# The tail of a mixture-of-experts layer: half of the rank rows added by accumulating transfers

## What is computed

```python
h = h + g2 * _moe(u, ...)          # routed experts + shared expert
return _rmsnorm(h, final_g)

# _moe: 128 experts, each token goes to its top 8
routed = sum over the token's 8 experts of weight * swiglu(u; expert)
return routed + _swiglu(u, shared_w_gu, shared_w_down)
```

## Time and profile before

| | us |
|---|---|
| median of three runs | 1250.67 |
| the profiled execution, its own time | 1252.62 |
| its span, first to last instruction | 1250.9 |
| TensorE busy | 1194.5 (95%) |
| VectorE busy | 699.6 (56%) |
| GpSimd busy | 322.5 (26%) |
| DMA over the span | 321.56 MB, 257 GB/s in the mean |

### The profile page before, as it was taken

How to read it: one execution, slowest core, us unless ns; L and a number is a source line. 1 busy time by engine, 2 the same in 40 slices (tenths; PEclk the granted TensorE clock), 3 DMA queues, 4 the chain that set the end, 5 groups by cost and what they waited for, 6 DMA issues and landing times.

```text
span 1250.9 us, 20127 instructions
## 1 busy us (share of the span) xinstructions
PE 1194.5 (95%) x5713; PEld 702.1 (56%) x5714; DVE 699.6 (56%) x1224; ACT 515.1 (41%) x598; POOL 322.5 (26%) x335
## 2 busy tenths in 40 slices
PE   5899999999999999998999999999999999999892
PEld 5688887777888888873443443443433434434341
DVE  3542447577562686858453444444444457667458
ACT  5572224755412413231344454454444445545211
POOL 1000000000000000014244544534434445455461
PEclk9799999999999999999999999999999999999896
DMA  9633503354393674746888799888888889999592
GB/s 332 213 107 115 183 1 103 108 193 167 115 376 132 207 267 149 230 176 236 350 323 329 301 333 328 311 330 316 317 322 320 327 322 362 413 409 407 239 422 90
DMA packets 88593, 321.56 MB, mean 257 GB/s; under 512 B 13040, under 2 KB 16344, under 8 KB 66152
## 3 DMA queue, kind: packets, MB, share of 16 engines
q1 hardware_dynamic: 69192, 279.69, 60.5%
q0 software_dynamic: 14432, 32.85, 7.0%
q10 hardware_dynamic: 4928, 8.49, 1.9%
HBM read 292.35 MB, written 48.24 MB: 272 GB/s over the span
## 4 chain that ended last, share of the span: by engine, by line
PE 87%; DVE 6%; ACT 2%; issue 2%; DMA 2%; DVEq 0%; SPq 0%; POOL 0%; POOLq 0%; ACTq 0%
PE psum L1670 33%; PE psum L1904 27%; PE psum L1914 13%; PE psum L1893 4%; PE psum L1643 2%; PE psum L1772 1%; PE psum L1943 1%; DMA ring<-in_ada_w 1%; PE psum L1703 1%; PE psum L1964 1%; DMA xT<-in_shared_w_down 1%; PE psum L1761 1%; PE psum L1732 1%; DVE stage L1619 1%; PE psum L1828 1%
## 5 line engine op out<-in xcount | busy, mean ns | idle before, releaser
L1904 PE MATMUL psum<-w_now,xT 128*64 128x512 f32 x1568 | 347.3, 595 | 0.6 <-DVE w_now L1518 0.6
L733 POOL COPY w_now<-stage 128x2048 f32 x79 | 150.1, 1917 | 275.5 <-PE psum L1914 229.6
L1904 PEld LDWEIGHTS psum<-w_now,xT 128*64 128x64 f32 x1568 | 108.7, 137 | 197.4 <-issue 196.2
L1914 PE MATMUL psum<-w_now,mask 128*64 128x512 f32 x784 | 176.6, 592 | 0.0
L1013 ACT ACTIVATE w_now<-stage 128x2048 f32 x79 | 147.7, 1907 | 39.1 <-issue 37.4
L468 DVE TENSOR_TENSOR w_lo<-ring,w_hi 128x1024 fp32r<-128x1024 f32 x80 | 94.7, 1222 | 84.7 <-ACT w_hi L461 82.8
L1670 PE MATMUL psum<-uT_hi,w_hi 128*128 128x512 f32 x352 | 139.3, 396 | 1.1 <-DVE w_lo L468 1.1
L1670 PE MATMUL psum<-uT_hi,w_lo 128*128 128x512 f32 x352 | 137.0, 389 | 0.0
L1670 PE MATMUL psum<-uT_lo,w_hi 128*128 128x512 f32 x352 | 137.0, 389 | 0.0
L461 ACT ACTIVATE w_hi<-ring 128x1024 fp32r<-128x1024 f32 x80 | 82.7, 1056 | 121.9 <-PE psum L1670 59.9
L680 POOL IOTA tok_cols<- 128x4 f32 x1 | 0.2, 158 | 509.6 <-PE psum L1670 509.6
(11 more groups left out here) (358 smaller groups left out, 1699.7 us busy)
## 6 DMA issues: line engine op xcount, KB each, us to landing
stage<-in_exp_w_gu SPq DMA_DIRECT2D x106, 1024.0 KB, 8.4
stage<-in_exp_w_down SPq DMA_DIRECT2D x53, 1024.0 KB, 7.9
ring<-in_w_in SPq DMA_DIRECT2D x56, 512.0 KB, 5.4
expert_rows<-zero_fill SPq DMA_DIRECT2D x16, 1024.0 KB, 8.2
ring<-in_ada_w SPq DMA_DIRECT2D x32, 512.0 KB, 5.0
stage<-expert_rows SPq DMA_DIRECT2D x12, 1024.0 KB, 20.8
ring<-in_ada_w SPq DMA_DIRECT2D x4, 1024.0 KB, 13.7
scale_w<-in_ada_w SPq DMA_DIRECT2D x4, 1024.0 KB, 14.4
```

Of the source, the lines that this page charges most:

```text
L733: pool.tensor_copy(w_now[:, q, 4:6], staged(turns[q] + STAGES - 1, 4, 2)).then_inc(dn_moved, 1)
L1904: mm = pe.matmul(moe_bank(GU)[at, :], xT[:, s % 2, k, at], gu_part(q, k), start=(k == 0), stop=(k == KT - 1))
L1914: mm = pe.matmul(moe_bank(Y0 + g)[at, :], hT[:, j, at], dn_part(q, j, g), start=(j == 0), stop=(j == 1))
```

## The change

SyncE loads ranks 0 to 3 only, in two transfers of 1 MB for each tile. As each lands, GpSimd issues a transfer that reads two of ranks 4 to 7 from DRAM and adds them onto the two ranks just loaded (ranks 4, 5 onto 0, 1, and ranks 6, 7 onto 2, 3), cut to pieces of 4 KB at most, and raising `slots_in[t][2 + g]`. GpSimd adds nothing itself and `ranks_summed` is gone. TensorE adds no ranks, and its order is another: the last block's `down_rows` comes first, then `shared_down` of tiles 0 and 1, then `last_rows` of both. VectorE waits for the first accumulating transfer, adds buffer 1 and the PSUM banks onto buffer 0, norms the tile before, waits for the second, and adds buffers 2 and 3; the rest is as it was.

```diff
@@ SyncE @@
-                for g, (first, end) in enumerate(rank_groups[t]):
+                for g, (first, end) in enumerate(rank_groups[t][:2]):
                     sp.dma_start(ranks_of(t, first, end - first), slot_rows[t][:, first:end]).then_inc(slots_in[t][g], 16)
@@ GpSimd @@
             for t in range(TT):
-                total = ranks_of(t, 0)
-                for r in (1, 2, 3):
-                    if r < 3:
-                        pool.wait_ge(slots_in[t][r - 1], 16)
-                    own(pool.tensor_tensor(total, total, ranks_of(t, r), ALU.add))
-                pool.nop().then_inc(ranks_summed, 1)
+                for g in range(2):
+                    pool.wait_ge(slots_in[t][g], 16)
+                    pool.dma_start(ranks_of(t, 2 * g, 2), slot_rows[t][:, 4 + 2 * g:6 + 2 * g], accum_op=ALU.add, max_dma_last_dim=4 * D).then_inc(slots_in[t][2 + g], 16)
@@ VectorE @@
             for t in range(TT):
-                acc = ranks_of(t, 0).rearrange("p o d -> p (o d)")
                 rank = lambda r: ranks_of(t, r).rearrange("p o d -> p (o d)")
-                dve.wait_ge(ranks_summed, t + 1)
+                acc = rank(0)
+
+                def add(part):
+
+                    own(tt(acc, acc, part, ALU.add))
+                    own.settle()
+
+                dve.wait_ge(slots_in[t][2], 16)
+                add(rank(1))
                 dve.wait_ge(some_summed, t + 1)
-                own(tt(acc, acc, psum[:, 2 * t:2 * t + 2, :].rearrange("p g n -> p (g n)"), ALU.add))
-                own.settle()
+                add(psum[:, 2 * t:2 * t + 2, :].rearrange("p g n -> p (g n)"))
                 if t:
                     normed(t - 1)
-                if rank_groups[t][3][0] == 6:
-                    dve.wait_ge(slots_in[t][3], 16)
-                else:
-                    dve.wait_ge(slots_in[t][2], 16)
-                own(tt(acc, acc, rank(6), ALU.add))
-                own.settle()
                 dve.wait_ge(slots_in[t][3], 16)
-                own(tt(acc, acc, rank(7), ALU.add))
-                own.settle()
+                add(rank(2))
+                add(rank(3))
@@ TensorE @@
-                    pe.matmul(psum[:, 2 * t + n, :], to_tokens[1][:, t], y_last[:, at], start=False, stop=False)
-
-            def add_ranks(t):
-
-                pe.wait_ge(slots_in[t][2], 16)
-                for n in range(2):
-                    for r in (4, 5):
-                        mm = pe.matmul(psum[:, 2 * t + n, :], ident[:], ranks_of(t, r)[:, 0, n * NC:(n + 1) * NC], start=False, stop=(r == 5))
+                    mm = pe.matmul(psum[:, 2 * t + n, :], to_tokens[1][:, t], y_last[:, at], start=False, stop=True)
                 mm.then_inc(some_summed, 1)
 
-            pe.wait_ge(shared_in[1], 16)
-            pe.wait_ge(xT_ready, live_n + 1)
-            pe.wait_ge(dve_emptied, emptied_by.count("dve"))
-            shared_down(0)
             pe.wait_ge(hT_ready, live_n)
             pe.wait_ge(dn_moved, copies)
             pe.wait_ge(y_ready, live_n + 1)
             down_rows()
-            shared_down(1)
+            pe.wait_ge(shared_in[1], 16)
+            pe.wait_ge(xT_ready, live_n + 1)
+            pe.wait_ge(dve_emptied, emptied_by.count("dve"))
+            for t in range(2):
+                shared_down(t)
             pe.wait_ge(to_tokens_ready, 2)
             pe.wait_ge(y_ready, live_n + 2)
-            last_rows(0)
-            add_ranks(0)
-            last_rows(1)
-            add_ranks(1)
+            for t in range(2):
+                last_rows(t)
             pe.wait_ge(idx_ready, live_n + AHEAD - 1)
             for t in (2, 3):
                 shared_down(t)
                 last_rows(t)
-                add_ranks(t)
```

More of the change, by code:

```diff
@@ L375, in layer_program @@
         zeros_out = sem("zeros_out")
-        ranks_summed = sem("ranks_summed")
         to_tokens_ready = sem("to_tokens_ready")
```

## The result

| | before | after |
|---|---|---|
| median of five runs, us | 1249.80 | 1258.95 |
| lowest to highest | 1248.14 to 1251.49 | 1257.69 to 1262.1 |
| the profiled execution, its own time | 1252.62 | 1262.1 |
| its span | 1250.9 | 1260.3 |
| SyncE loads the final norm's row at | 1170.6 | 1173.6 |

The ratio is 1.0075, with a 95% interval of 1.0062 to 1.0088: the change made the kernel 0.75% slower, some 9 us. The tail of the two profiled executions differs by 6.4 us. The changed kernel's started 3.0 us later, which is in every block of the expert loop alike (2.97 to 3.07 us at the 35 scatters from 608 to 1012 us), so that it comes from before the loop, in code that the change doesn't touch.

What follows compares the result with a forecast made beforehand. VectorE bounds the tail before, the transfer stream after: 1202.8 + 40.1 (eight accumulates) + 1.3 + 0.5 = 1244.7, plus 11.0 for VectorE's end and store = 1255.7, 4.8 over the span; as measured time 1255.5, range 1240 to 1280.

Steps and rivals of the forecast that it cites:

- The price of an accumulate, twice a plain load: Tail's DMA stream: each 1.049 MB accumulating transfer takes 5.0 us, against 2.50 for a plain load.
- Rival B: Tail's transfers: read, add and write follow each other, an accumulate costs over 2.5 plain loads; 1275.8 at three; chance 0.20.
- rival A: Tail's transfers: the destination's read is mostly hidden, an accumulate costs under 1.57 plain loads; end 1235 to 1247; chance 0.27.
- The ports: Tail's transfers: if writing into SBUF limits a plain load, an accumulate's second read comes nearly free.
- The stream, to 1244.7 by the clock of the first profile: Tail's transfers: plain loads to 1202.8, eight accumulates 40.1 us, tile 1's result 1.3, landing and waking 0.5.
- VectorE turned from the bound into the one that waits: Tail: the transfers' 16.1 us of slack is spent, and VectorE waits for accumulating transfers, lastly at `slots_in[3][3]`.
- GpSimd's issue hidden, 1 to 3 us each: Tail: issuing the accumulating transfers takes GpSimd 8 to 24 us in all, hidden beside 40 us of transfers.
- Rival C: Tail: GpSimd's issue of accumulating transfers binds, from 7.8 us each on; end 1264 at 9 us each; chance 0.03.
- Tile 0's sum at 1194.5, `down_rows` from 1177.3: TensorE in the tail: `down_rows` starts when hT is ready, bringing tile 0's sum to about 1194.5 instead of 1201.2.
- The baseline: The profiled span of 1250.9 us, which the forecast end of 1255.7 was set against, giving 4.8 us slower.
- By VectorE alone, 1235: Tail if transfers kept up: 1194.5 plus 7.5, 27.0, 3.0 for root and norm, 3.0 for the store; 15.9 below 1250.9.
- The line 1215.6 + 20.05 f: End of the span in us, f being an accumulate's price in plain loads; equal to before at f = 1.76.

Runs made afterwards that it cites:

- experiment 3: The changed kernel with four more accumulating transfers of 1 MB, into buffers that nobody reads: ratio 1.0235, median 1279.61 us.
- experiment 2: The changed kernel with pieces of 8 KB in place of 4 KB in the accumulating transfers: ratio 1.0075, median 1258.84 us.
- experiment 8: The kernel before with only TensorE's changed order (the last block's `down_rows` first, then `shared_down` of tiles 0 and 1): ratio 0.9978, median 1248.57 us.
- Experiment 1: The changed kernel, its eight GpSimd transfers without the add, so ranks 4 to 7 overwrite ranks 0 to 3: ratio 0.9968, median 1246.17 us.
- experiments 10 to 12: Kernel before, VectorE adding rows as they land, no GpSimd adds: 0.9966; plus TensorE's new order, later `h` loads: 0.9966; plus TensorE adding tile 3's ranks 6, 7: 0.9953.
- experiment 9: The changed kernel with four accumulating transfers (ranks 6, 7 onto 2, 3); SyncE loads ranks 4, 5 and TensorE adds them: ratio 0.9999, median 1249.98 us.
- experiment 7: The kernel before, GpSimd waiting as it did but adding nothing, ranks 1 to 3 left out: ratio 0.9947, median 1243.29 us.

## Why the prediction was right, and its sum too small

It forecast the side, the mechanism and the size of the main term. The measured time, 1258.95, lies in the range; the change was forecast at +4.8 us and measured at +9.2, so that the sum had little more than half of it.

- *The price of an accumulate, twice a plain load.* Right: 2.03 in the stretch of the changed kernel where they run alone, 1.97 by the occupied time of the same packets with and without the add, 5.25 us each where four are added. Rival B (over 2.5) falls with it, and so does rival A (under 1.57). The row that the prediction took it from could not give it: from 345 to 362 us loads run beside stores, and no transfer there adds. The runs show that the engines are occupied twice as long; that this is the second read is the reading that fits, and no run here takes the read and the add apart. The Trainium skill ("Collectives: The Full Stack", The bandwidth ceiling: the fold count and why AG ≠ RS ≠ AR) has a ratio of 1.93 for collectives; these traces agree with it within some 5%, for a transfer whose second operand lies in SBUF.
- *The ports.* The other page that the prediction weighed ("DMA: Bandwidth & Descriptors" of the Trainium skill, Where 436 GB/s comes from, the SBUF ports as the bottleneck) says what limits a plain load; what the prediction drew from it, that the second read would be nearly free, did not come true: at 206 GB/s of sums, accumulating transfers write into SBUF at half the rate of plain loads, with the engines full.
- *The stream, to 1244.7 by the clock of the first profile.* Right but short. The last transfer landed 75.6 us behind the start of the tail, forecast at 74.1. The term is the eight accumulates: 40.1 us in the sum, 40.7 at 206 GB/s and 42.0 at experiment 3's price.
- *Four operations and 11.0 us to the end.* Right: 11.1.
- *VectorE turned from the bound into the one that waits.* Right: 36.6 us of waits in eight places. Its adds are all 1.2 us, and its waits are where the prediction wanted them, ahead of every half tile.
- *GpSimd's issue hidden, 1 to 3 us each.* Right, 1.2 us. Rival C, which needed 7.8 us each, falls: experiment 2 made the issue 0.35 us shorter and nothing moved.
- *Tile 0's sum at 1194.5, `down_rows` from 1177.3.* Off: I looked at hT alone. `down_rows` also waits for `dn_moved`, GpSimd's last copy of weights, 4.0 us more, and then takes 6.4 us instead of 3.6, the granted clock being 0.68 in the stretch from 1178 to 1185 and 0.77 from 1185 to 1190. It ends at 1188.2, which is 1185.2 by the clock of the first profile and not 1181. Tile 0's sum comes at 1195.5 by that clock, 1.0 us late. In the changed kernel VectorE waits for transfers at that time and it cost nothing; in the kernel before, the new order alone is worth 2.7 us by the runs (experiment 8).
- *The baseline.* This is where most of the rest most likely lies. The sum was made against one execution's tail of 80.3 us, as if it were the kernel's, and that execution, 1252.62, was slower than all five timed ones (at most 1251.49). The stretching of VectorE by GpSimd's adds, which I had read off at six operations, is not the same in each execution: another profile shows a tail of 77.6. Of the 9.2 us, 4.8 were in the sum, 1.6 are the stream's price and the end (the tails of the two first profiles differ by 6.4), and up to 2.7 are the shorter tail that the kernel before can have; what is left is within the interval. That the timed executions had the shorter tail is argued and not shown: none of them was profiled.
- *"By VectorE alone, 1235".* Wrong, though it decided only rival A's price. Experiment 1 is that case, plain transfers in place of accumulating ones, and its tail is 72.1 us and not 64.4. VectorE's operations were counted from the first sum on as if their rows were there, and they land at the stream's pace: 7.5 us of waits. The line 1215.6 + 20.05 f thus doesn't hold at its lower end: at f = 1 it gives 1235.7, and experiment 1, moved to the first profile's start of the tail, 1242.7. Rival A would have gained less than it was priced at.

## What to carry to other kernels

An add inside a transfer was not free while the DMA engines were full: it cost as much as a second transfer of the same bytes. Before work is moved from an engine to the stream, set the stream's own slack (here 16 us) against the price (here 20 to 22 us), and look whether the engine that is to be relieved could not rather start earlier: adding each row as it lands, with nothing new in the stream, gained 4 to 6 us here (experiments 10 to 12). And where a tail has several limits within a few microseconds, take the baseline from more than one profile and ask which limit comes next, because each one removed gave only the distance to the next.

## What the runs showed of the hardware that was not expected

- An accumulating transfer's packets occupy the DMA engines for twice as long as plain ones of the same size (42.5 against 21.6 us for 8.66 MB), and longer pieces hardly change it: 41.2 us, and a tail of 86.2 us in place of 86.7.
- A plain load that shares the engines with accumulating transfers of another queue can be held up long: 38 us from issue to landing in experiment 9, 30 and more in the changed kernel, against 25 to 27 us for tile 3's loads before, although SyncE's queue then held more plain loads (16 of ranks, against 12 and 8).
- What GpSimd's adds cost VectorE differs between executions of one kernel: six of its operations took some 3.3 us instead of 1.2 in two profiles of the kernel before, and five in the third; with the other order of TensorE and the same adds it was four (experiment 8). With no add on GpSimd none was stretched (experiment 7).
